# Stores, gate rows and queries cross two block borders in a hybrid decoder step

## The reference

```python
q = rope(q_raw.reshape(b, s, NSA_HEADS, HEAD_DIM), pos)
gates = jax.nn.sigmoid(g_raw.astype(F32)).reshape(b, s, 3, NSA_HEADS)
kv = kv_raw.reshape(b, s, 6, NSA_KV_HEADS, HEAD_DIM)
new_kv = jnp.stack([k_cmp, kv[:, :, 1], k_slc, kv[:, :, 3]], axis=2)   # an output
new_win = jnp.stack([k_win, kv[:, :, 5]], axis=2)                      # its last rows: an output
kc = nsa_compress(full_kv[:, :, 0], pe[0], w1[0], w2[0])   # silu(blocks of 32 rows @ w1) @ w2
vc = nsa_compress(full_kv[:, :, 1], pe[1], w1[1], w2[1])
# three branches (compressed, selected, window), each softmax(q k) v, then
o = g[:, :, 0] * o_c + g[:, :, 1] * o_s + g[:, :, 2] * o_w
```

## Time and profile before

| | us |
|---|---|
| median of 3 runs | 1769.04 |
| lowest and highest run | 1766.49, 1770.69 |
| the profiled execution, first to last instruction | 1768.3 |
| TensorE busy in it | 1627.3 |
| idle of TensorE at the first, second and third meeting | 6.21, 4.29, 5.99 |

### The profile page before, as it was taken

How to read it: one execution, slowest core, us unless ns; L and a number is a source line. 1 busy time by engine, 2 the same in 40 slices (tenths; PEclk the granted TensorE clock), 3 DMA queues, 4 the chain that set the end, 5 groups by cost and what they waited for, 6 DMA issues and landing times. The chain is left out here.

```text
span 1768.3 us, 26601 instructions
## 1 busy us (share of the span) xinstructions
PE 1627.3 (92%) x11217; PEld 1249.5 (71%) x11217; DVE 763.0 (43%) x1256; ACT 579.5 (33%) x1109; POOL 358.5 (20%) x236
## 2 busy tenths in 40 slices
PE   4999898899999899999999959998999999998798
PEld 4445567576666689999978747885999975554485
DVE  3221111266666666650188844323321444445543
ACT  4102111265545542222245533324421312222221
POOL 1111000011000012221379734110220200000231
PEclk8999998899999999999989979998999999998899
DMA  9222163222121011111011164113000120002621
GB/s 327 98 83 48 62 174 83 75 72 89 49 87 46 14 29 42 43 48 48 17 36 31 43 172 167 60 51 90 25 25 24 43 102 1 25 24 84 241 96 66
DMA packets 119676, 129.88 MB, mean 73 GB/s; under 512 B 16728, under 2 KB 91914, under 8 KB 119430
## 3 DMA queue, kind: packets, MB, share of 16 engines
q1 hardware_dynamic: 118950, 127.56, 22.7%
q0 software_dynamic: 608, 0.63, 0.3%
HBM read 107.05 MB, written 23.18 MB: 74 GB/s over the span
## 5 line engine op out<-in xcount | busy, mean ns | idle before, releaser
L154 PE MATMUL banks<-h_T_rest,w_ssd_high 128*128 128x352 f32 x480 | 156.0, 325 | 0.0
L154 PE MATMUL banks<-h_T_high,w_ssd_high 128*128 128x352 f32 x480 | 155.8, 325 | 0.0
L154 PE MATMUL banks<-h_T_high,w_ssd_rest 128*128 128x352 f32 x480 | 155.2, 323 | 0.0
L154 PE MATMUL banks<-w_attn,h_T 128*128 128x408 f32 (+5 forms) x432 | 148.3, 540 | 2.6 <-DVE h_T L570 2.6
L154 PEld LDWEIGHTS banks<-w_attn,h_T 128*128 128x128 f32 (+1 forms) x432 | 74.4, 182 | 74.8 <-issue 52.6
L154 PE MATMUL banks<-w_r,h_T 128*128 128x512 f32 (+1 forms) x320 | 116.4, 550 | 0.0
L1306 DVE TENSOR_REDUCE pe_T<-banks 128x1 f32<-128x512 f32 (+7 forms) x108 | 81.9, 765 | 38.2 <-PE banks L154 37.5
L154 PE MATMUL banks<-out_even_w_high,mix_high 128*128 128x512 f32 (+1 forms) x216 | 86.7, 401 | 12.5 <-DVE out_even_w_rest L2237 12.5
L1223 ACT ACTIVATE p_att<-banks,pe_T 128x512 f32<-128x512 f32 (+7 forms) x128 | 86.2, 680 | 16.2 <-DVE pe_T L1306 15.2
L154 PEld LDWEIGHTS banks<-h_T_high,w_ssd_rest 128*128 128x128 f32 x480 | 90.9, 189 | 0.0
L154 PEld LDWEIGHTS banks<-h_T_high,w_ssd_high 128*128 128x128 f32 x480 | 90.2, 188 | 0.6 <-issue 0.6
(11 more groups left out here) (487 smaller groups left out, 3468.3 us busy)
## 6 DMA issues: line engine op xcount, KB each, us to landing
w_mod_late<-in_w_mod_dram SPq DMA_DIRECT2D x8, 2048.0 KB, 7.8
w_ssd<-in_w_in_even_dram SPq DMA_DIRECT2D x20, 512.0 KB, 3.6
w_mod_rows<-in_w_mod_dram SPq DMA_DIRECT2D x4, 2048.0 KB, 20.2
xin<-in_x_prompt_dram SPq DMA_DIRECT2D x8, 512.0 KB, 10.1
cmp_w<-in_nsa_cmp_w_dram SPq DMA_DIRECT2D x8, 512.0 KB, 7.5
silu_z_T<-in_state_ssd_dram SPq DMA_DIRECT2D x8, 512.0 KB, 4.2
out_dram<-silu_z_T SPq DMA_DIRECT2D x8, 512.0 KB, 3.5
out_even_x_rows<-in_x_prompt_dram SPq DMA_DIRECT2D x8, 512.0 KB, 3.6
```

Source lines behind the costliest of these rows:

```text
L154: return nc.tensor.matmul(out, lhsT, rhs, start=start, stop=stop, skip_group_check=True)
```

## The change

The projection block keeps only the save of the gates on SP, which now waits for the first pass of key/value copies alone (`kv_freed` at `NT`). The eleven stores come at the end of SP's list in the page block. There, behind the last page and ahead of the third part of `cmp_w1`, SP also loads the 24 gate rows, after waiting for the saved gates (`g_saved`). POOL clears `QS` at the start of the page block, DVE fills it behind the 16 pages. DVE's copies of the compressed values go to the start of the sample block; the samples' compressed values are in banks 2 and 3 instead of 0 and 1, and TensorE's transposes wait for the copies (`v_cmp_taken`). The wait for the stored sample results goes from the end of the sample block to the head of SP's list in the prompt block. `QS`, `grow` and `acc` live in a place that reaches across the blocks.

```diff
@@ -438,17 +438,8 @@
                 for hh in range(HG):
...
                         sp.dma_start(A.w_za[:, :, hh * P + g * HD:hh * P + (g + 1) * HD], wv[:, :, (g * HG + hh) * HD:(g * HG + hh + 1) * HD]).then_inc(A.w_za_in, 16)
-                sp.wait_ge(rot_done, 3 * NT)
-                sp.wait_ge(kv_freed, 2 * NT)
-                kv = A.kvrow
-                sp.dma_start(e.outs[2][0, 0].rearrange("(m p) a g d -> p m (a g d)", p=P), kv[:, 0:NTP, 0:512]).then_inc(rows_out, 16)
-                sp.dma_start(e.outs[3][0].rearrange("b t a g d -> (b t) (a g d)"), kv[0:TS, NTP, 0:512]).then_inc(rows_out, 16)
-                sp.dma_start(e.outs[4][0, 0].rearrange("(m p) a g d -> p m (a g d)", p=P),
-                             kv[:, NTP - WIN // P:NTP, 512:768]).then_inc(rows_out, 16)
-                for b in range(DB):
-                    sp.dma_start(e.outs[5][0, b, PAST - DS:PAST].rearrange("t a g d -> t (a g d)"),
-                                 kv[b * DS:(b + 1) * DS, NTP, 512:768]).then_inc(rows_out, 16)
-                sp.dma_start(e.g_save, A.gates[0:TS, NTP, :]).then_inc(rows_out, 16)
+                sp.wait_ge(kv_freed, NT)
+                sp.dma_start(e.g_save, A.gates[0:TS, NTP, :]).then_inc(A.g_saved, 16)
 
...
             def _(pe):
@@ -647,12 +638,13 @@
         w1, w2 = sb("cmp_w1", [P, 2, CB // 2, 2 * HD]), sb("cmp_w2", [P, 2, HD])
...
+        A.QS, A.grow = sb("q_block_diagonal", [P, DB, G, HG * DS]), sb("gate_rows", [P, 2, 3])
...
         with nc.Block() as block:
...
             def _(sp):
@@ -672,9 +664,23 @@
                         load_w1(0)
...
                         sp.dma_start(w2[:, :, :], e.nsa_cmp_w2[0].rearrange("v h d -> h v d")).then_inc(w2_in, 16)
+                kv, rows_out = A.kvrow, e.stored["kv_rows"]
+                sp.wait_ge(A.g_saved, 16)
+                for f in range(2):
+                    for br in range(3):
+                        for b in range(4):
+                            src = e.g_save.rearrange("(b t) (a h) -> b a h t", t=DS, a=3)[4 * f + b, br].rearrange("h (t x) -> h t x", x=1)
+                            sp.dma_start(A.grow[32 * b:32 * (b + 1), f, br:br + 1], src, allow_slow_non_contiguous=True).then_inc(A.g_in, 16)
                 for n in range(2, 4):
...
                     load_w1(n)
+                sp.dma_start(e.outs[2][0, 0].rearrange("(m p) a g d -> p m (a g d)", p=P), kv[:, 0:NTP, 0:512]).then_inc(rows_out, 16)
+                sp.dma_start(e.outs[3][0].rearrange("b t a g d -> (b t) (a g d)"), kv[0:TS, NTP, 0:512]).then_inc(rows_out, 16)
+                sp.dma_start(e.outs[4][0, 0].rearrange("(m p) a g d -> p m (a g d)", p=P),
+                             kv[:, NTP - WIN // P:NTP, 512:768]).then_inc(rows_out, 16)
+                for b in range(DB):
+                    sp.dma_start(e.outs[5][0, b, PAST - DS:PAST].rearrange("t a g d -> t (a g d)"),
+                                 kv[b * DS:(b + 1) * DS, NTP, 512:768]).then_inc(rows_out, 16)
 
...
             def _(pe):
@@ -718,7 +724,7 @@
                 for b in range(DB):
...
                         at = (b % 4) * P + g * HD
-                        last = mm(nc, e.ps[0:NCS, b // 4, at:at + HD], hid[:, 1, g, NCP + b * NCS:NCP + (b + 1) * NCS], w2[:, 1, :], True, True)
+                        last = mm(nc, e.ps[0:NCS, 2 + b // 4, at:at + HD], hid[:, 1, g, NCP + b * NCS:NCP + (b + 1) * NCS], w2[:, 1, :], True, True)
                 last.then_inc(cmp_done, 1)
...
             @block.scalar
@@ -737,6 +743,7 @@
 
...
             def _(pool):
+                nc.gpsimd.memset(A.QS[:, :, :, :], 0.0).then_inc(q_zeroed, 1)
                 pool.wait_ge(tr_done, NP)
...
 
@@ -748,14 +755,13 @@
                     src = e.ps[:, i % 2, 0:256].rearrange("p (v n c) -> p v n c", v=2, c=CB)
...
                                             ALU.add).then_inc(tr_dve, 1)
+                dve.wait_ge(q_zeroed, 1)
+                for g in range(G):
+                    nc.vector.tensor_copy(A.QS[g * HD:(g + 1) * HD, :, g, :].rearrange("p b (h t) -> p b h t", t=DS),
+                                          A.QT[g * HD:(g + 1) * HD, :, TP:T].rearrange("p h (b t) -> p b h t", t=DS))
+                dve.wait_ge(zeroed, 1)
                 dve.wait_ge(cmp_done, 1)
-                dve.wait_ge(zeroed, 1)
                 nc.vector.tensor_copy(A.kccT[:, :], e.ps[:, 6, 0:NKEY // CB])
-                for h in range(HG):
-                    nc.vector.tensor_copy(A.vcd[h * 32:(h + 1) * 32, :, h * HD:(h + 1) * HD],
-                                          e.ps[h * 32:(h + 1) * 32, 7, 0:128].rearrange("p (g d) -> p g d", g=G))
-                nc.vector.tensor_copy(A.vcs[:, 0:4, :], e.ps[0:NCS, 0, :].rearrange("p (b d) -> p b d", b=4))
-                nc.vector.tensor_copy(A.vcs[:, 4:8, :], e.ps[0:NCS, 1, :].rearrange("p (b d) -> p b d", b=4))
     end_block(nc)
...
 
@@ -768,14 +774,14 @@
...
-        QS = sb("q_block_diagonal", [P, DB, G, HG * DS])
+        QS = A.QS
...
@@ -798,27 +804,19 @@
                 sp.dma_start(numbers[:, :], e.page_table.rearrange("b n -> (b n)").rearrange("(a n) -> a n", a=1)).then_inc(pt_in, 16)
...
                 load_values(sp, 0)
-                sp.wait_ge(e.stored["kv_rows"], 16 * (2 * DB + 4))
-                for f in range(2):
-                    for br in range(3):
-                        for b in range(4):
-                            src = e.g_save.rearrange("(b t) (a h) -> b a h t", t=DS, a=3)[4 * f + b, br].rearrange("h (t x) -> h t x", x=1)
-                            sp.dma_start(grow[32 * b:32 * (b + 1), f, br:br + 1], src, allow_slow_non_contiguous=True).then_inc(g_in, 16)
+                sp.wait_ge(e.stored["kv_rows"], 16 * (2 * DB + 3))
                 for f in range(2):
...
                         dst = e.o_save.rearrange("(b t) (h d) -> b h t d", t=DS, d=HD)[4 * f + b]
-                        sp.dma_start(dst, acc[32 * b:32 * (b + 1), f, :]).then_inc(o_out, 16)
-                sp.wait_ge(o_out, 16 * DB)
+                        sp.dma_start(dst, acc[32 * b:32 * (b + 1), f, :]).then_inc(A.o_saved, 16)
 
...
             def _(pool):
-                nc.gpsimd.memset(QS[:, :, :, :], 0.0).then_inc(zeroed, 1)
                 load_values(pool, 1)
...
             def _(pe):
-                pe.wait_ge(q_ready, 1)
                 for f in range(2):
...
                     for br in range(2):
@@ -839,6 +837,7 @@
                     z_product(nc, e, A, x, z_bank(x)).then_inc(z_done, 1)
...
                 gate(Z_EARLY)
+                pe.wait_ge(v_cmp_taken, 1)
                 for f in range(2):
...
                     for br in range(2):
@@ -879,11 +878,12 @@
             @block.vector
...
                 link = make_link(dve, e.dve_step, e.dve_n)
-                dve.wait_ge(zeroed, 1)
-                for g in range(G):
-                    last = nc.vector.tensor_copy(QS[g * HD:(g + 1) * HD, :, g, :].rearrange("p b (h t) -> p b h t", t=DS),
-                                                 A.QT[g * HD:(g + 1) * HD, :, TP:T].rearrange("p h (b t) -> p b h t", t=DS))
-                last.then_inc(q_ready, 1)
+                for h in range(HG):
+                    nc.vector.tensor_copy(A.vcd[h * 32:(h + 1) * 32, :, h * HD:(h + 1) * HD],
+                                          e.ps[h * 32:(h + 1) * 32, 7, 0:128].rearrange("p (g d) -> p g d", g=G))
+                for x in range(2):
+                    last = nc.vector.tensor_copy(A.vcs[:, 4 * x:4 * x + 4, :], e.ps[0:NCS, 2 + x, :].rearrange("p (b d) -> p b d", b=4))
+                last.then_inc(v_cmp_taken, 1)
                 for f in range(2):
...
                     nc.vector.tensor_reduce(mx[:, f, 0:1], e.ps[:, 4 * f, NK:NK + NCS], AX.X, ALU.max)
@@ -896,7 +896,7 @@
                         nc.vector.tensor_copy(pT[:, f, br, 0:PAST], e.ps[:, 4 * f + 2 + br, 0:PAST])
...
                     nc.vector.tensor_copy(pcT[:, f, :], e.ps[0:NCS, 4 * f + 2, 384:512]).then_inc(pt_ready, 1)
-                dve.wait_ge(g_in, 16 * 24)
+                dve.wait_ge(A.g_in, 16 * 24)
                 link(nc.vector.reciprocal(den[:, :, :], den[:, :, :]))
...
                 for f in range(2):
@@ -1045,6 +1045,7 @@
         with nc.Block() as block:
...
             def _(sp):
+                sp.wait_ge(A.o_saved, 16 * DB)
                 for g in range(G):
...
                     sp.dma_start(dst, e.o_save[:, g * HG * HD:(g + 1) * HG * HD].rearrange("t (h d) -> t h d", d=HD)).then_inc(o_smp_in, 16)
@@ -2294,11 +2295,14 @@
             A.peT, A.kccT = sb("pe_T", [P, 2 * CB]), sb("k_cmp_T", [P, NKEY // CB])
...
                 A.pages = [first]
+            with nc.sbuf_tensor("acc_samples", [P, 2, HD], F32) as A.acc:
+                pass
             A.o_smp = sb("o_samples", [TS, H * HD])
...
             A.vcs = sb("v_cmp_samples", [NCS, DB, P])
+            A.g_saved, A.g_in, A.o_saved = (nc.alloc_semaphore(s) for s in ("gates_saved_samples", "gate_rows_in", "o_samples_saved"))
```

10 lines of the change are left out of this document (5 added, 5 removed).

## The result

| | before, us | changed, us |
|---|---|---|
| median of 4 runs each, side by side | 1767.76 | 1745.68 |
| lowest and highest run | 1765.27, 1770.69 | 1743.61, 1747.35 |
| the profiled execution | 1768.3 | 1742.0 |
| TensorE busy in it | 1627.3 | 1606.9 |

What follows compares the result with a forecast made beforehand. TensorE, busy 1627.3 of 1768.3 us, bounds it; time can come from idle stretches and low clock. Terms 5.3 - 0.5 + 3.2 + 3.4 + 4.7 + 1.9 = 18.0 us, with 0.7 added: 1751.0; range 1747 to 1758.

Steps and rivals of the forecast that it cites:

- The first meeting: Projection to page block: with stores moved, its end goes from SP's 218.27 to ACT's 213.25, gaining 5.3 us.
- The term of -0.5 for the page block: Page block: a longer wait for page 6 may bring a longer slow stretch, costing 0.5 us.
- Gate rows and stores: Page block: gate-row loads at 0.73 us hidden, 1.4 us left; eleven stores end 6.4 us before DVE; no cost.
- SP ends late: Second meeting, page to sample block: stores dearer behind weights, SP 4 us late, clock lost, 1758.4 us; chance 7%.
- the slower rival: Page block: gate-row loads at 2.25 us each hold up the third weight load, 1786 us; chance 3%.
- The second meeting and its clock: Page to sample block: TensorE starts 3.2 us earlier, and the clock kept up behind it saves 3.4 us.
- some tenths: Sample block: at full clock, DVE's value copies may end this much later than TensorE's first-half scores.
- The third meeting: Sample to prompt block: no DVE wait for gate rows, no SP wait for landing; ACT ends last, gaining 4.7 us.
- 1.00 behind each: Sign in the changed profile: granted clock at this level behind each of the three meetings.
- bound for ACT's exponentials alone: Prompt block start: kept-up clock saves 3.9 us at most; 1.9 taken, as ACT's eight exponentials are next late.
- From the prompt block on I expect the same program, shifted: From the prompt block to the end: same program, only shifted, with a forecast saving of 0.
- the lower end of the range: Whole kernel: 1747 us, taken from the bounds of the clock terms.

Runs made afterwards that it cites:

- the kernel with eight weight parts: Changed kernel with compression weights issued four pages later, in eight 0.5 MB parts with four buffers instead of four parts with two: 1742.57 us, ratio 0.9852.
- third part alone: Kernel before with only the gate rows loaded in the page block and the sample stores' landing awaited in the prompt block: 1762.65 us, ratio 0.9952.
- second part alone: Kernel before with only the queries built in the page block and the value copies moved to the sample block: 1766.04 us, ratio 0.9980.
- the later weights: Changed kernel with the first two compression weight loads and the small third one issued behind pages 8 and 9, not 4 and 5: 1745.74 us, ratio 0.9862.
- first part alone: Kernel before with only the eleven kv stores moved behind the weight loads of the page block: 1765.08 us, ratio 0.9973.

## Why the prediction was right or wrong

**The first meeting: right.** 5.1 us against 5.3, and the stores alone move it. The term of -0.5 for the page block was right in the first profile (52.2 to 52.7) and too small by half in the others, where stretch 2 takes 53.1 and 53.2: page 6 waits for 4.23, 3.67 and 4.16 us, inside the 3.5 to 5 that the prediction gave, with a clock of 0.72, 0.57 and 0.72 over the 6 us behind it. In two of three executions of the changed kernel the clock also fell briefly behind the first meeting itself. That costs nothing, for the reason given there: TensorE waits for page 6 anyway.

**Gate rows and stores: right.** 0.70 us each instead of 0.73, 2.1 us of room instead of 1.4, and the eleven stores end 4.4 us ahead of DVE where 6.4 were expected. As a group they take 2.1 us longer than they did in the projection block. The rival "SP ends late" was nearer than I thought and still had 4.4 us to go. The experiment with the stores ahead of the weights shows the slower rival's mechanism; its condition, dearer gate rows, did not come about.

**The second meeting and its clock: right.** 3.1 us against 3.2, and 3.6 against 3.4. The clock stays at 1.00 behind the meeting in all nine executions of kernels that have this part, their stretch 4 being 16.8 to 16.9 us each time. The copies end 0.3 us or so behind the scores of the first half, the forecast "some tenths". What the prediction did not say is that this part is worth only half alone. It counted the parts as a sum, and so would have given 6.6 us for the second alone, where 3.5 were measured and 1.7 are left in the six stretches of its trace.

**The third meeting: right in size, and for one of two reasons only.** 4.7 us as forecast, with ACT last. The prediction named two moved things, the gate rows and the landing. The rows carry it (9.5 us lost without them, clock included). With the rows early the landing is worth nothing: the meeting's idle is 1.31 us with and without it. With the rows late it was worth 0.8 us. The clock of "1.00 behind each" was wrong here: it is 0.79 in all three executions of the changed kernel. The term still came out at 1.7 against 1.9. I had halved its bound for ACT's exponentials alone, and at 333.01 TensorE does wait 0.82 us for them, but part of what the halving covered was a lower clock that I hadn't foreseen. That the size fits is partly luck.

**What failed.** The step is the sentence "From the prompt block on I expect the same program, shifted", together with the lower end of the range, which was made of the clock terms beside the meetings alone. I put the rest of the program at nothing, without a reason beyond its being the same program. In the profiled pair it is 8.6 us faster, 5.2 of them in stretch 7. The program there is the same, its clock isn't. The kernel before was profiled three times and had the slow stretch near 888 us each time (597.4, 597.2, 597.4 us for stretch 7); the changed kernel was profiled three times and had it once (596.8, against 592.2 and 591.7). I had the earlier trace rows with a clock of 0.59 behind 1.8 us of idle time, took it as a model for the meetings, and did not ask whether that stretch itself would stay.

Nor is the slow stretch 7 all of it: the third profile, without it, has the second slow place instead, and its stretch 8 is 547.7 us against 543.4 in the first. Averaged over the three profiles of each kernel, the six stretches save 16.6 us (16.2 to 17.7 by profile) and the rest 3.6; together 20.3 from the unrounded spans, where the 13 and 41 runs show 20.7. So the 8.6 us of the first pair were a lucky execution, and 3.6 us are what the prediction's zero left out on average.

The second half of the miss is the sample. The four runs that the change was first compared with had the median 1745.68; the nine of the other two comparisons have the medians 1751.02 (five runs) and 1750.63 (four). The forecast of 1751.0 is 2.5 us above the median of all, and 1745.68 is the low one of three medians of the same kernel.

**What stays open.** Whether the change makes the slow stretch 7 rarer, or chance did. Over all experiments, of nine executions with the second part of the change seven lack it (the two with it are the repeat of the changed kernel and the kernel with eight weight parts), and all five without that part have it, the kernels with the first or the third part alone among them. The kernel with the second part alone lacks it. As an estimate, if the part had no influence, a split as clean as this would come up in one case of 95 (the ways to place the five among the seven that have the stretch, against all ways to place them among fourteen); but the question was put after the rows were seen. Against a firm link to the second part speaks that one of the six runs of the kernel with the third part alone took 1755.99 us at a mean clock of 0.975, where the other five took 1760.64 to 1765.12 at 0.965 to 0.969; that run has no trace, but it looks like one without the stretch. The idle time ahead is 1.79 to 1.81 us in all traces that I read it in, with the stretch and without, so no row shows how a shift of some us upstream would decide it. Many more profiles of the same two kernels would be needed, and that was not tried.

Four of the seven executions without the slow stretch 7 have the second slow place instead (the third profile of the changed kernel, the kernels with the landing kept, with the stores ahead and with the later weights), none of the others has it, and in these four stretch 8 is 547.5 to 548.7 us where it is 543.4 to 545.6 in the other ten. So a missing slow stretch 7 is often paid back there, and why is open too.

## What to carry to other kernels

Where all engines meet, ask which one arrives last and move that engine's work; then price the next-latest chain before counting the gain, since a gain on TensorE is lost whole if another queue still ends last (the second part alone gave 3.5 us, not 6.6). A queue that waits for a buffer has room for other issues of its own, up to the time at which the buffer comes free and not one us more; measure that room, and put the rest behind the transfer that somebody waits for. And give the range room for the slow stretches in parts that the change doesn't touch: a shifted program is the same work, but not the same clock.

## What the runs showed of the hardware

- **One program, nine microseconds.** The changed kernel's 13 runs reach from 1743.61 to 1752.77 us, and the mean granted clock of a run goes with its time: 0.976 to 0.980 in the four below 1746.5 us, 0.968 to 0.974 in the nine above. The program is the same in all of them; three of the 13 have a trace, and these three differ in whether and where a slow place of 4 to 5 us comes.
- **The same idle time, either clock.** Behind 1.80 us of idle time the granted clock was 1.00 in the stretch (3.79 us for 32 products) or 0.59 (6.86 us for the same 32); behind 1.06 us at the first meeting 1.00 (1.06 us for eight transposes) or 0.73 in the stretch. Behind the 1.16 or 1.17 us at the second meeting it never fell in nine executions. Near the program's end the same 105 recorded matmuls lay in 14.8 us with a clock of 0.96 in one execution of the changed kernel and in 19.1 us with 0.58 in another. A single profile shows one of the outcomes and doesn't say how likely it is.
- **Transposes run at the full clock.** Eight transposes of 128x128 fp32 in 1.06 us with a clock of 1.00 directly behind the first meeting, 1.94 us in the earlier trace rows, in a stretch with 0.50.
- **The price of a small store goes with what is queued ahead.** The store of the samples' rows (L678) took 2.69 us of SP's time behind 1 MB of weights in the changed kernel, 2.88 behind them in the kernel with the first part alone, which has no gate rows there, and 0.58 behind the gate rows in the kernel that has the stores ahead of the weights. The price of a store read at another place in a queue was too low by 2 us for this one, and by 2.1 for the eleven together.
